# Ln and Exp from their joint table set, and table loads placed by hand, in a one-core kernel of eleven stages

## What is computed

```python
def dn_prepare(qkv, ab, conv_w, a_log, dt_bias):          # delta inputs
    t = jax.nn.silu(dwconv(qkv, conv_w)).astype(jnp.float32)
    q = l2norm(t[..., :DN_QK_W]...) * DN_DK ** -0.5
    k = l2norm(t[..., DN_QK_W:2 * DN_QK_W]...)
    g = -jnp.exp(a_log) * jax.nn.softplus(ab[:, :, 0] + dt_bias)
    beta = jax.nn.sigmoid(ab[:, :, 1])

def rmsnorm(s, g):                                        # delta norm, and the norms
    return (s32 * lax.rsqrt(jnp.mean(s32 * s32, axis=-1, keepdims=True) + EPS)) * g
```

## Time and profile before

| | us |
|---|---|
| median of 3 runs | 3797.59 |
| lowest, highest | 3795.94, 3798.28 |
| the profiled execution | 3804.48 |
| its span, first to last instruction | 3803.2 |

### The profile page before, as it was taken

How to read it: one execution, slowest core, us unless ns; L and a number is a source line. 1 busy time by engine, 2 the same in 40 slices (tenths; PEclk the granted TensorE clock), 3 DMA queues, 4 the chain that set the end, 5 groups by cost and what they waited for, 6 DMA issues and landing times.

```text
span 3803.2 us, 72363 instructions
## 1 busy us (share of the span) xinstructions
PE 3532.9 (93%) x31740; PEld 2276.7 (60%) x31740; DVE 1675.3 (44%) x2942; ACT 1181.9 (31%) x2157; POOL 1393.0 (37%) x1239
## 2 busy tenths in 40 slices
PE   7999899999999989898999998999888888889998
PEld 3755584344554555554555554456667677658887
DVE  1245562366531234444333425524666666433344
ACT  3154342322214633413000002114666556320002
POOL 1230550133312245665323333344444444144443
PEclk9999899999999989999999999999999999999999
DMA  5441005311112135301111211331000000122221
GB/s 190 133 137 34 2 14 178 127 47 54 49 49 68 45 111 177 134 23 52 59 56 56 66 51 50 105 112 51 17 17 17 17 17 3 55 70 89 89 89 67
DMA packets 196435, 263.78 MB, mean 69 GB/s; under 512 B 6135, under 2 KB 151671, under 8 KB 194072
## 3 DMA queue, kind: packets, MB, share of 16 engines
q1 hardware_dynamic: 188960, 241.74, 19.2%
q10 hardware_dynamic: 7160, 17.41, 1.2%
HBM read 246.55 MB, written 12.58 MB: 68 GB/s over the span
## 4 chain that ended last, share of the span: by engine, by line
PE 53%; ACT 6%; DVE 4%; issue 4%; POOL 1%; DMA 0%; ACTq 0%; DVEq 0%; SPq 0%; POOLq 0%
PE ps L238 42%; PE ps L3238 2%; PE ps L771 2%; ACT mem L848 1%; PE ps L382 1%; PE ps L798 1%; PE ps L786 1%; PE ps L489 1%; DVE mem L829 1%; PE ps L3757 1%; POOL mem L3540 0%; PE ps L498 0%; PE ps L3765 0%; ACT mem L858 0%; ACT mem L3173 0%
## 5 line engine op out<-in xcount | busy, mean ns | idle before, releaser
L238 PE MATMUL ps<-mem 64*64 64x64 f32 (+4 forms) x25120 | 2624.0, 295 | 98.4 <-ACT mem L3173 26.1
L238 PEld LDWEIGHTS ps<-mem 64*64 64x64 f32 (+1 forms) x25120 | 1704.2, 150 | 1025.4 <-issue 519.6
L3103 POOL TENSOR_TENSOR mem<-mem 128x256 f32<-128x256 f32 (+1 forms) x264 | 228.2, 878 | 342.6 <-ACT mem L3650 176.8
L866 POOL TENSOR_SCALAR mem<-mem 128x768 f32<-128x768 f32 (+2 forms) x128 | 219.3, 1727 | 202.7 <-DVE mem L832 202.7
L2366 ACT ACTIVATE mem<-ps 128x384 f32<-128x384 f32 (+1 forms) x80 | 35.7, 446 | 779.1 <-PE ps L238 736.8
L2353 POOL TENSOR_TENSOR mem<-mem 128x512 f32<-128x512 f32 (+1 forms) x80 | 100.9, 1261 | 445.2 <-PE ps L238 368.4
L596 POOL TENSOR_TENSOR mem<-mem 128x512 f32<-128x512 f32 (+1 forms) x72 | 75.3, 1064 | 417.5 <-ACT mem L591 414.3
L2377 DVE TENSOR_TENSOR mem<-mem,ps 128x384 f32<-128x384 f32 (+1 forms) x80 | 39.9, 499 | 415.8 <-PE ps L238 415.8
L3238 PE MATMUL ps<-mem 128*128 128x128 f32 x960 | 166.4, 289 | 26.6 <-DVE mem L3162 14.0
L3162 DVE TENSOR_TENSOR mem<-mem,ps 128x256 f32<-128x256 f32 (+1 forms) x220 | 109.6, 514 | 110.8 <-PE ps L238 109.9
L3171 ACT ACTIVATE mem<-ps 128x256 f32<-128x256 f32 (+1 forms) x220 | 101.5, 462 | 173.3 <-PE ps L3238 173.0
(11 more groups left out here) (339 smaller groups left out, 4082.7 us busy)
## 6 DMA issues: line engine op xcount, KB each, us to landing
mem<-i_mod_w SPq DMA_DIRECT2D x48, 1024.0 KB, 6.9
mem<-i_ffn_wg SPq DMA_DIRECT2D x22, 1024.0 KB, 5.3
mem<-i_ffn_wu SPq DMA_DIRECT2D x22, 1024.0 KB, 5.3
mem<-i_e_w_in SPq DMA_DIRECT2D x16, 1024.0 KB, 6.2
mem<-i_o_w_in SPq DMA_DIRECT2D x16, 1024.0 KB, 5.4
mem<-i_ffn_wd SPq DMA_DIRECT2D x16, 1024.0 KB, 4.9
mem<-i_e_mod_w SPq DMA_DIRECT2D x12, 1024.0 KB, 11.8
mem<-i_o_mod_w SPq DMA_DIRECT2D x12, 1024.0 KB, 6.6
```

Of the source, the lines that this page charges most:

```text
L238: ins = e.h.matmul(out, l, r, start=(i == 0), stop=(i == n - 1))
L866: K.pool.h.tensor_scalar(w, w, stat(i, o, 1), None, MUL).then_inc(*nm.up(tag, i, o))
L3103: K.pool.h.tensor_tensor(m3(self.slot(l)), self.lraw, bm(C(K, f"cm{self.d}", l, 64), 2 * self.np), MUL).then_inc(*self.mk.up(key, l))
```

## The change

Four helpers load a table set by its name: `log_and_exp` (the set with both Ln and Exp), `logs` (Ln), `silus` and `sigmoids`. They are called

- in `Norm.roots`, `logs` in the place of the Ln on one column;
- in the delta inputs, `silus` ahead of the wait for the convolution and `log_and_exp` behind the Square of each q and k tile, behind the Sigmoid of the gates, and at j = 12;
- `log_and_exp` behind the four Silus of `z_act`, `silus` ahead of the waits in the gates and the FFN;
- in the projections of the RWKV block, `sigmoids` ahead of "rw" and `log_and_exp` behind "rg";
- in `front_act`, `sigmoids` behind Ln and Exp, `log_and_exp` behind each direction's Sigmoids, and `sigmoids` behind the Exp of direction 0.

The program had 188 table loads and has 141. No other instruction changes but the nine Ln on one column, which are gone; on the other engines the order is the same, and no wait is added or taken away.

```diff
--- before.py
+++ after.py
@@ -64,6 +64,9 @@
         return self
 
     def activation(self, *_, **k):
+        return self
+
+    def preload_act_table_set(self, *_):
         return self
 
     def tensor_tensor(self, *_, **k):
@@ -614,7 +617,7 @@
 
     def roots(self):
         K, tag = self.K, self.tag
-        K.act.h.activation(K.spare, C(K, "eps")[:, ONE:ONE + 1], ACT.Ln).then_inc(*self.sqs.up(tag, "table"))
+        logs(K)
         R = self.sets()[:len(self.R)]
         for i, (name, r0, rn, *_) in enumerate(R):
             K.act.wait_ge(*self.sm.at(tag, *name))
@@ -667,6 +670,26 @@
         K.pe.wait_ge(*out.at(tag, 1 if r0 else 0, k))
         return dst(k, r0, rn)
     return normed
+
+
+def log_and_exp(K):
+
+    K.act.h.preload_act_table_set("natural_log_exp_and_others")
+
+
+def logs(K):
+
+    K.act.h.preload_act_table_set("natural_log")
+
+
+def silus(K):
+
+    K.act.h.preload_act_table_set("silu_and_others")
+
+
+def sigmoids(K):
+
+    K.act.h.preload_act_table_set("sigmoid_and_others")
 
 
 def modulate(K, A, B):
@@ -1197,6 +1220,8 @@
                 K.act.h.activation(rr[:, 0:n], rr[:, 0:n], ACT.Exp, scale=-0.5).then_inc(*nrm.up(i, "r"))
             if j < 12:
                 n = ranges(j)[-1][0] + ranges(j)[-1][1]
+                if kind(j) != "v" or kind(j - 1) != "v":
+                    silus(K)
                 K.act.wait_ge(*conv.at(j, len(ranges(j)) - 1, 4))
                 K.act.h.activation(c[:, 0:n], c[:, 0:n], ACT.Silu).then_inc(*sil.up(j, 0))
                 if kind(j) != "v":
@@ -1204,6 +1229,9 @@
                     if j >= 3:
                         K.act.wait_ge(*ones.at(j - 3, len(ranges(j - 3)) - 1))
                     K.act.h.activation(sq[j % 3][:, 0:n], c[:, 0:n], ACT.Square).then_inc(*sil.up(j, 1))
+                    log_and_exp(K)
+            elif j == 12:
+                log_and_exp(K)
             next(beside, None)
 
     def dve():
@@ -3033,6 +3065,8 @@
                 post(k, ri, u[:, k, r0:r0 + rn]).then_inc(*nrm.up("m0", ri, k))
         K.act.h.dma_start(K.spill, K.xt).then_inc(*sp_.up(by=16))
         for n, (tag, j, _, cols, rngs, to) in enumerate(jobs):
+            if tag == "rw":
+                sigmoids(K)
             if n in units:
                 for i, unit in enumerate(units[n]):
                     unit.first()
@@ -3057,6 +3091,8 @@
                 K.act.wait_ge(*out.at(tag, i))
                 K.act.h.dma_start(K.rkv[m][:, to + r0:to + r0 + rn], buf).then_inc(*st[t % 4].up(t, by=16))
                 t += 1
+            if tag == "rg":
+                log_and_exp(K)
         return t
 
     def sp(t):
@@ -3456,11 +3493,14 @@
                     A.wait_ge(*(fd.at(hp, 0, "q0") if d else fd.at(hp - 1, 1, "q0")))
                     A.wait_ge(*(fa.at(hp, 0, "wc") if d else fa.at(hp - 1, 1, "wc")))
                 A.h.activation(ep[:, r0:r0 + rn], K.ps[self.banks(hp, f"w{d}")[ri]][:, 0:rn], ACT.Sigmoid, bias=PVC(K, "w0", d * 8 + hp)).then_inc(*fa.up(hp, d, "w", ri))
+            log_and_exp(K)
             yield
             yield
             A.wait_ge(*fd.at(hp, d, "sum", 1))
             A.h.activation(ep, en, ACT.Exp, scale=-EXPH).then_inc(*fa.up(hp, d, "ep"))
             A.h.activation(en, en, ACT.Exp, scale=EXPH).then_inc(*fa.up(hp, d, "en"))
+            if d == 0:
+                sigmoids(K)
             yield
             A.wait_ge(*fd.at(hp, "kk"))
             A.h.activation(m3(self.lane[d]["kkt"])[:, :, 63 - c:64 - c], m3(self.kk)[:, :, 63 - c:64 - c], ACT.Copy).then_inc(*fa.up(hp, d, "kkt"))
```

## The result

The changed kernel takes 3774.11 us (median of six runs, 3769.3 to 3783.14) beside 3797.38 us for the kernel before on the same chip: 23.3 us less, ratio 0.9938 with a 95% interval of 0.9927 to 0.9949. The forecast was 3782.3 us with a range of 3774 to 3790, so the direction was right and the gain half as large again as forecast. The interval of the ratio reaches from 19 to 28 us, and 15.3 lies outside it. The time stands at the very edge of the wide range, and outside the 3777 to 3788 that the forecast gave itself. Rows of both are used.

What follows compares the result with a forecast made beforehand. PE was taken as the bound, so only loads ahead of its waits counted: -11.1 - 0.6 + 0.5 - 3.2 - 0.9 = -15.3 us, from the median 3797.6 to 3782.3 us, range 3774 to 3790.

Steps and rivals of the forecast that it cites:

- Rival 4: A load directly behind an activation costs about as much again, as ACT's pipe drains first; 3800 us, chance 2%.
- Delta inputs and L1449: Shorter PE waits for the Square in the delta inputs, -11.1 us; earlier first Exp of the delta scan, -0.6.
- z_act: Ahead of the delta norm, the load behind the last Silu delays DMA issues and PE: +0.5 us, or nothing.
- Finish: End of each RWKV head pair: without the second load, PE's waits of 0.94 and 0.35 go, -1.29 us a pair.
- key norms: RWKV scan's front: one load instead of two ahead of copies that PE waits for, -1.28 us a pair.
- Direction 0: RWKV scan's front: the load for Exp, now ahead of four inverse copies, falls wholly on PE, +1.3 us a pair.
- Direction 1: RWKV scan's front: a 1.28 us load ahead of copies that wait 0.50 for PE costs the rest, +0.8 a pair.
- Sigmoid load in direction 0: RWKV scan's front: put ahead of already late inverse copies, this load adds nothing or 0.1 us.
- Sum of a pair: RWKV scan: finish, key norms and both directions together give -0.46 us a head pair, -3.2 us for seven.
- rival 1: Displaced copies in the scan cost nothing, since the inverse has slack; scan gives 18 us, 3767.5 us, chance 7%.
- Tail: Last pair's finish loses the load ahead of Exp, so SP issues the projection's weights earlier: -0.9 us.
- Edits at nothing: One-column Ln and loads ahead of waits in gates, FFNs, "rw" and "rg": no PE time gained or lost.

Runs made afterwards that it cites:

- f_sig_at_use: The changed kernel with direction 1's Sigmoid load put back directly ahead of its Sigmoids; ratio 0.9936 to the kernel before.
- e_exp_at_use: The changed kernel with only the scan's loads for Exp put back directly ahead of Exp, in both directions; ratio 0.9938 to the kernel before.
- b_only_scan: The kernel before with the edits of the RWKV scan alone; ratio 0.9956 to the kernel before.
- d_at_use: The changed kernel with all the scan's loads put back to directly ahead of the Exp or Sigmoids that need them; 3771.33 us, ratio 0.9912 to the kernel before.
- after2: The changed kernel again with no edit, for a second profile; 3781.26 us beside 3805.24 for the kernel before, ratio 0.9932.
- before2: The kernel before again with no edit, for a second profile; ratio 1.0009.
- h_two_loads_d0: The changed kernel with a Silu set load added ahead of the joint set's load behind direction 0's Sigmoids; ratio 0.9956 to the kernel before.

## Why the prediction was right and wrong

- **What a load costs**: right. 1.28 us with gaps of 0.01 to 0.02 around it, also where it is loaded by name and right behind an ACTIVATE. Rival 4's drain is not in these traces: the Sigmoids ahead of the load at 2810.95 end at 2809.88 + 1.05 = 2810.93. The Trainium skill's "ScalarE: Activation LUTs" states that drain in "What ACT_TABLE_LOAD costs", 1.38 us; the trace does not agree.
- **Delta inputs and L1449, -11.7**: right, with some luck in the number. The part alone measured 11.8; the waits and the projections went as written, the clock there with them. But the 11.1 was worked out from one profile of before; by the second the stage gains 10.2. And 1.5 us of clock at the delta scan's start were not in the sum.
- **z_act, +0.5**: wrong, 0. The text had left open whether an issue needs a free datapath and took the dearer answer; the issue doesn't wait for the load, which lies under it.
- **Finish, -1.29, and key norms, -1.28**: right, 1.37 and 1.28 measured.
- **Direction 0, +1.3**: this step failed. A load ahead of copies was put down with its full length, since the copies "did not wait". In the kernel before these copies stood at PE's pace, 0.65, 0.56 and 0.66 us apart; held up by a load, they follow each other every 0.48 us, so that PE is only 0.94 late. The mechanism was named (the whole load stands ahead of four copies); the size was off by 0.36 us a pair.
- **Direction 1, +0.8**: the same step, and the same omission. At the load's own level PE is 0.41 late. The whole step takes 0.31 in pair 2 and 0.55 on average, with waits in it that the load doesn't explain.
- **Sigmoid load in direction 0, 0 to 0.1**: right where it stands (f_sig_at_use); e_exp_at_use shows that it depends on the other load.
- **Sum of a pair**: -1.40 in pair 2 and -1.3 on average at full clock, not -0.46. The seven pairs with their clock are -6.6 and not -3.2, which is 3.4 of the 8 us that the forecast missed. The direction of the error is that of rival 1, at about half of its way (it had 2.57 a pair): it was dismissed because the lanes have no slack, which was true, but slack was not the only thing that could shrink the bill.
- **Tail, -0.9**: right. The wait for rwkv_wo is 0.87 and 0.64 us in the two profiles of before; it is gone in the first profile of the changed kernel and in b_only_scan, and 0.25 in the second.
- **Edits at nothing**: right, 1.0003.

The sum with measured terms is -11.1 - 0.6 - 1.5 + 0 - 6.6 - 0.8 = -20.6 us; measured are 23.3, and 24 to 26 in the other two sittings. The missing 3 to 5 us have no row of their own. A thousandth of PE's mean clock goes with 3.5 us from run to run, so they are within it. Whether the changed kernel is also granted a little more clock on average (0.975, 0.974 and 0.975 in its three sittings, before 0.9725 and 0.974 in two) can't be told from these runs: shorter waits went with it in the delta inputs, where the rows show it, and beyond them nothing here settles it.

## What to carry to other kernels

A load put ahead of short instructions that ran at another engine's pace costs less than its length (0.94 of 1.28 us here), because they close up behind it; read their spacing in the trace, both waiting and queued, not their durations, and count that rebate once. Judge two moved loads around one pair of handovers together: here each edit alone read as nothing, where d_at_use gave 8 us. When one table set covers both functions of a chain, name that set at every place that could evict it: the one line left out here was worth as much (22 to 24 us) as the whole change (23 to 26).

## What the runs showed of the hardware that was not expected

- Start to start, ACTIVATEs of 0.60 us whose inputs lie ready follow each other every 0.47 to 0.50 us, behind a load (after2, 2812.24 to 2813.69) and behind an Exp (before2, 2837.01 and 2837.48); at PE's pace they are up to 0.66 us apart.
- A DMA issue on ACT's queue starts while a table load is running, 0.74 us into its 1.28 (rows of the changed kernel at 593.22 and 593.96).
- Of two equal table loads in a row the build keeps one; with another set between, both run, 1.28 us each (2812.57 and 2813.86 in h_two_loads_d0, PE's wait 1.97 us).
- The 5 us around a wait of PE of 2.17 us had a mean granted clock of 0.66; every 5 us of pair 2 in the changed kernel's second profile, with waits of 0.68 and 0.73 in the same places, had 1.00. Runs of one program spread by 14 us with a mean clock from 0.973 to 0.977.
